# Two layers' mixer inputs, gated recurrence, pooling and difference attention put into one stage

## What is computed

```
for l in range(2):
    u = rms_norm(h, norm1_g[l])
    p_in, dq, dk, dv, gq, gk, gv, gr, gg = split(u @ w_in[l])   # 256, 512, 512, 512, 128, 128, 256, 256, 16 columns
    y_pool = (causal means of p_in over 2, 4, 8, 16 tokens - p_in) @ pool_w * pool_scale
    y_diff = rms_norm((softmax(q0 k0) - lam * softmax(q1 k1)) @ v) * gain   # 4 heads, two maps of 64, values of 128,
                                                                            # mask by blocks of 64 tokens
    y_gla  = rms_norm(chunked gated recurrence of gq, gk, gv with log decays from gg) * silu(gr)
                                                                            # 4 heads, keys 32, values 64, chunks of 64
    h = h + concat(y_pool, y_diff, y_gla) @ w_out[l]
    h = h + square(relu(rms_norm(h) @ w_mlp1[l])) @ w_mlp2[l]
```

## Time and profile before

| | |
|---|---|
| median of 3 runs | 2982.12 us (2980.08 to 2985.23) |
| the profiled execution, its own time | 2992.76 us |
| its span in the profile | 2991.0 us |
| instructions | 45324 |
| PE, DVE, ACT, POOL busy | 2706.6, 1510.7, 1001.0, 274.0 us |
| weight load part of PE (PEld) busy | 2131.9 us |
| DMA | 222.99 MB, mean 75 GB/s |

### The profile page before, as it was taken

The page is one execution under the profiler, slowest core; times in us unless marked ns, Lnnn a source line. Parts: engine busy times, 40 slices in busy tenths (PEclk is TensorE's granted clock), DMA queues, the critical chain, the costliest instruction groups (busy, mean ns, idle before and its releaser), DMA issues. The chain is left out here.

```text
span 2991.0 us, 45324 instructions
## 1 busy us (share of the span) xinstructions
PE 2706.6 (90%) x19410; PEld 2131.9 (71%) x19410; DVE 1510.7 (51%) x1980; ACT 1001.0 (33%) x1600; POOL 274.0 (9%) x217
## 2 busy tenths in 40 slices
PE   6989999799997999899999946999999966899998
PEld 4745688678886787688787834778777854687776
DVE  4654598345676233566534356552443347553443
ACT  3333575333333222333333225321222225331221
POOL 0210001312320000111111020100001020100000
PEclk8999999768999999999999978999999978999999
DMA  6224211000003233233222200223222200232322
GB/s 237 64 88 131 89 62 57 3 3 3 4 32 118 92 93 113 76 92 98 79 93 90 92 8 3 90 92 92 92 86 91 92 21 1 72 98 85 92 91 71
DMA packets 64712, 222.99 MB, mean 75 GB/s; under 512 B 7168, under 2 KB 7552, under 8 KB 64384
## 3 DMA queue, kind: packets, MB, share of 16 engines
q1 hardware_dynamic: 63360, 216.94, 22.9%
q10 hardware_dynamic: 1152, 3.15, 0.3%
HBM read 213.77 MB, written 6.29 MB: 74 GB/s over the span
## 5 line engine op out<-in xcount | busy, mean ns | idle before, releaser
L276 DVE TENSOR_TENSOR w_lo<-ring,w_hi 128x1024 fp32r<-128x1024 f32 (+1 forms) x339 | 420.9, 1242 | 984.0 <-ACT w_hi L268 983.9
L268 ACT CAST w_hi<-ring 128x1024 fp32r<-128x1024 f32 (+1 forms) x339 | 353.2, 1042 | 1115.2 <-PE ps L298 995.4
L298 PE MATMUL ps<-u_hi,w_hi 128*128 128x512 f32 x1104 | 441.0, 399 | 15.0 <-DVE u_lo L493 10.1
L298 PE MATMUL ps<-u_hi,w_lo 128*128 128x512 f32 x1104 | 437.4, 396 | 0.0
L298 PE MATMUL ps<-u_lo,w_hi 128*128 128x512 f32 x1104 | 435.7, 395 | 0.0
L298 PE MATMUL ps<-mid_hi,w_hi 128*128 128x512 f32 x688 | 275.1, 400 | 16.8 <-PEq L2609 10.6
L298 PE MATMUL ps<-mid_lo,w_hi 128*128 128x512 f32 x688 | 275.3, 400 | 0.0
L298 PE MATMUL ps<-mid_hi,w_lo 128*128 128x512 f32 x688 | 274.4, 399 | 0.0
L298 PEld LDWEIGHTS ps<-u_hi,w_hi 128*128 128x128 f32 x1104 | 208.1, 188 | 71.8 <-issue 17.7
L298 PEld LDWEIGHTS ps<-u_hi,w_lo 128*128 128x128 f32 x1104 | 208.2, 189 | 52.4
L298 PEld LDWEIGHTS ps<-u_lo,w_hi 128*128 128x128 f32 x1104 | 208.1, 189 | 49.9
(11 more groups left out here) (390 smaller groups left out, 4524.1 us busy)
## 6 DMA issues: line engine op xcount, KB each, us to landing
ring<-in_w_up SPq DMA_DIRECT2D x44, 512.0 KB, 3.5
ring<-in_w_in SPq DMA_DIRECT2D x42, 512.0 KB, 3.5
ring<-in_w_mod_rest SPq DMA_DIRECT2D x32, 512.0 KB, 3.5
ring<-in_w_merge SPq DMA_DIRECT2D x32, 512.0 KB, 3.5
ring<-in_w_mlp1a SPq DMA_DIRECT2D x32, 512.0 KB, 3.5
ring<-in_w_mlp2a SPq DMA_DIRECT2D x32, 512.0 KB, 3.5
ring<-in_w_mlp1b SPq DMA_DIRECT2D x32, 512.0 KB, 3.5
ring<-in_w_mlp2b SPq DMA_DIRECT2D x32, 512.0 KB, 3.5
```

The lines of the kernel that those rows point to most:

```text
L268: nc.scalar.copy(w_hi[:, slot, 0:width], ring[:, n % RING, 0:width]).then_inc(*hi_ok.one())
L276: nc.vector.tensor_tensor(w_lo[:, slot, 0:width], ring[:, n % RING, 0:width], as_f32(w_hi[:, slot, 0:width]), ALU.subtract).then_inc(*lo_o ...
L298: mm = nc.tensor.matmul(dst[:, a:b], w[wi][:, k * P:(k + 1) * P], src[xi][:, k0 + k, a:b], start=start and k == wi == xi == 0, stop=stop a ...
```

## The change

The three stages become one, `stage_mixer`. The units' order changes to gg, gk, gq, gv (2), dv (4), then dk and dq of each head, pool input (2), gr (2). The pieces of recurrence, attention and pooling are placed between units and between quarters of a unit on TensorE's queue: gate matmul after unit 2 (counting from 0), transposes of the decayed keys after unit 6, recurrence scores after 7, states after 8, output inside unit 10; then ten **slots**, one per unit 11 to 20, in each of which one pair of attention items starts and the pair before ends; pooling stands in the last slot.

The operations change too. Keys and queries of the recurrence are used by their 32 partitions instead of through zeroed tiles, states have 64 columns instead of 256, the score products of the attention contract over 64 partitions each and their masks cover 64 columns over 32 partitions. The attention's values come token-major, one product per item; the norms of both mixers become sums along a row (`accum_out` of a Square on ScalarE, or a reduce on VectorE) with square roots of a few columns, and the normed tiles are transposed back by TensorE through one PSUM bank (bank 2) and scaled as ScalarE takes them out. The scaling by 1/16 moves into the Exps, the probabilities take one VectorE operation instead of two, and 1/sum of map 0 is applied when the value product is taken out. Transposed probabilities, back transposes and pool mixing take turns in bank 2, value products in bank 3, scores in banks 4 to 7. On ScalarE's and VectorE's queues the steps are written out in one order with the splits: in a slot ScalarE does split, both copies of transposed probabilities, first value copy and square, Exps of the first starting item, second value copy and square, Exps of the second; VectorE scales the last product, ends the second item's probabilities, splits, takes both maxima and ends the first item's probabilities. The updates of x in layer 0 move behind the first splits. GpSimd zeroes only small tiles, and its pool means go by tile, after cumulative sums that VectorE makes in slots 7 and 8.

```diff
         for layer in range(DEPTH2):
+            part, at_unit = {}, 0
+            for kind, n in (("pin", 2), ("gq", 1), ("gk", 1), ("gr", 2), ("gg", 1), ("dq", DH2), ("dk", DH2),
+                            ("gv", 2), ("dv", 4)):
+                part[kind] = t_w[f"in2_{layer}"][at_unit:at_unit + n]
+                at_unit += n
+            by_head = [part[kind][h:h + 1] for h in range(DH2) for kind in ("dk", "dq")]
+            t_w = {**t_w, f"in2_{layer}": sum([part["gg"], part["gk"], part["gq"], part["gv"], part["dv"]] + by_head +
+                                              [part["pin"], part["gr"]], [])}
...
-        def stage_mixer_inputs(u, x, first_gain, rstd, pin, gq, gk, gr, gg, qz, dk, dv, gv):
...
-        def stage_pool_gla(layer, mats, pin, gq, gk, gr, gg, gv, mix):
...
-                        nc.gpsimd.memset(kp[:], 0.0).then_inc(*l_ok.one())
...
-                        for half in range(2):
-                            nc.vector.tensor_scalar(kt[:, half, :, :].rearrange("p t c -> p (t c)"), ps[:, 3, :],
-                                                    tab("half", half, 1), None, ALU.mult).then_inc(*d_ok.one())
...
-        def stage_diff(layer, qz, dk, dv, mix):
...
+        def stage_mixer(layer, u, x, first_gain, rstd, mats, mix):
...
+            GG, GK, GQ, HEAD = 0, 1, 2, 9
+            FIRST = HEAD + 2
+            SLOTS = n_units - FIRST
...
+                        def gla_scores():
+
+                            for t in range(TL):
+                                for h in range(4):
+                                    r = slice(32 * h, 32 * h + 32)
+                                    mm = nc.tensor.matmul(ps[:, SCORE_BANKS[h], t * P:(t + 1) * P],
+                                                          kinv[r, t * P:(t + 1) * P], gq[r, t * P:(t + 1) * P],
+                                                          start=True, stop=True)
...
+                        def gla_states():
+
+                            for c in range(NCH):
+                                t, r = c // 2, slice(64 * (c % 2), 64 * (c % 2) + 64)
+                                for h in range(4):
+                                    mm = nc.tensor.matmul(ps[32 * h:32 * h + 32, STATE_BANKS[c % 2], 64 * t:64 * t + 64],
+                                                          kt[r, t, 32 * h:32 * h + 32], gv[r, t, 64 * h:64 * h + 64],
+                                                          start=True, stop=True)
...
+                        def gla_out():
+
+                            for t in range(TL):
+                                for h in range(4):
+                                    r, dst = slice(32 * h, 32 * h + 32), ps[:, OUT_BANKS[h], 64 * t:64 * t + 64]
+                                    nc.tensor.matmul(dst, at_[:, t, h, :], gv[:, t, 64 * h:64 * h + 64],
+                                                     start=True, stop=False)
+                                    for half in range(2):
+                                        c, q = 2 * t + half, slice(64 * half, 64 * half + 64)
+                                        mm = nc.tensor.matmul(dst[q, :], gq[r, c * GLA_C:(c + 1) * GLA_C], st[r, c, :],
+                                                              start=False, stop=True)
...
+                            def product_of_map(m):
+                                r = slice(64 * m, 64 * m + 64)
+                                nc.tensor.matmul(score(i, m), dq[r, h, t * P:n], dk[r, h, 0:n], start=True, stop=False)
+
+                            def masked(m):
+                                return nc.tensor.matmul(score(i, m)[:, n - 64:n], tab("mask_q")[0:32, :],
+                                                        tab("mask_k")[0:32, 64:128], start=False, stop=True)
+
+                            product_of_map(0)
+                            product_of_map(1)
+                            masked(0)
+                            masked(1).then_inc(*s_ok.one())
...
+                        def values(i):
+
+                            h, t = divmod(i, TL)
+                            pe.wait_ge(*tev.at(i + 1))
+                            if i > 0:
+                                pe.wait_ge(*o_ok.at(i))
                             for k in range(t + 1):
+                                mm = nc.tensor.matmul(ps[:, 3, t * P:(t + 1) * P], pt[:, i % 2, k * P:(k + 1) * P],
+                                                      dv[:, k, h * P:(h + 1) * P], start=k == 0, stop=k == t)
+                            mm.then_inc(*pv_ok.one())
...
+                        for n in range(3):
+                            part(unit(pe), n, 0, KD)
...
+                        pe.wait_ge(*rs_ok.at(1))
...
+                        pe.wait_ge(*evac.at(1))
+                        nc.tensor.matmul(ps[:, 0, :], mats[0:16, layer * P:(layer + 1) * P], gg[0:16, :],
+                                         start=True, stop=True).then_inc(*p_ok.one())
...
+                            if i == 1:
+                                pe.wait_ge(*d_ok.at(9))
+                                for t in range(TL):
+                                    mm = nc.tensor.transpose(ps[:, 0, t * P:(t + 1) * P], ke[:, t * P:(t + 1) * P], ident)
+                                mm.then_inc(*p_ok.one())
+                            elif i == 2:
+                                pe.wait_ge(*evac.at(2))
+                                pe.wait_ge(*tok_evac.at(4))
+                                pe.wait_ge(*a_ok.at(6))
+                                gla_scores()
+                            elif i == 3:
+                                pe.wait_ge(*d_ok.at(11))
+                                gla_states()
+                        pe.wait_ge(*d_ok.at(13))
+                        part(unit(pe), HEAD, 0, KD)
+                        w = unit(pe)
+                        part(w, HEAD + 1, 0, 2)
+                        pe.wait_ge(*d_ok.at(20))
+                        pe.wait_ge(*tok_evac.at(8))
+                        gla_out()
+                        part(w, HEAD + 1, 2, KD)
+                        for s in range(SLOTS):
+                            n = FIRST + s
+                            ending, starting = items_ending(s), items_starting(s)
+                            w = unit(pe)
+                            pe.wait_ge(*evac.at(feature(n) - 1))
+                            part(w, n, 0, 2)
+                            if ending:
+                                turn(ending[0])
+                            part(w, n, 2, 4)
+                            if starting:
+                                scores(starting[0])
+                            if ending:
+                                turn(ending[1])
+                                values(ending[0])
+                            elif s == SLOTS - 1:
+                                pool_mix(0)
+                            part(w, n, 4, 6)
+                            if starting:
+                                scores(starting[1])
+                            if ending:
+                                values(ending[1])
+                            elif s == SLOTS - 1:
+                                pool_mix(1)
+                            part(w, n, 6, KD)
+                            if s in (2, 4):
+                                gla_back((s - 2) // 2)
+                            elif s % 2 == 1 and s > 1:
+                                head_back((s - 3) // 2)
...
-                    with ExitStack() as s3:
...
-                        stage_mixer_inputs(u, x, (lambda n: vec("final", n)) if layer == 0 else None, rstd,
-                                           pin, gq, gk, gr, gg, qz, dk, dv, gv)
-                        normed.close()
-                        stage_pool_gla(layer, mats, pin, gq, gk, gr, gg, gv, mix)
-                        stage_diff(layer, qz, dk, dv, mix)
+                    stage_mixer(layer, u, x, (lambda n: vec("final", n)) if layer == 0 else None, rstd, mats, mix)
+                    normed.close()
```

More of the change, by code:

```diff
@@ L2455, in _, with part @@
                     @block.tensor
                     def _(pe):
-                        pe.wait_ge(*lam_ok.at(1))
-                        nc.tensor.matmul(ps[:, 7, 0:2], ones, lam[:, 0:2], start=True,
-                                         stop=True).then_inc(*lams_ok.one())
+                        def part(w, n, k0, k1):
+                            for k in range(k0, k1):
+                                for wi, xi in ((0, 0), (0, 1), (1, 0)):
+                                    mm = nc.tensor.matmul(ps[:, bank(n), :], w[wi][:, k * P:(k + 1) * P], u[xi][:, k, :],
+                                                          start=k == wi == xi == 0, stop=k == KD - 1 and wi == 1)
+                            if k1 == KD:
+                                mm.then_inc(*unit_used.one())
@@ new lines, in head_back, with pool_mix @@
+                        def head_back(h):
```

(31 more changed lines are left out.)

783 lines of the change are left out of this document (371 added, 412 removed).

## The result

| | before | after |
|---|---|---|
| median, runs taken side by side | 2982.25 us (2980.08 to 2985.23, 4 runs) | 2842.34 us (2837.21 to 2846.40, 4 runs) |
| the profiled execution, its own time | 2992.76 us | 2841.74 us |
| its span | 2991.0 us | 2840.0 us |

The ratio of after to before is 0.9529, 95% interval 0.9512 to 0.9547: faster, as predicted, 139.9 us by the medians against the 151.6 forecast. The two profiled executions differ by 151.0 us.

A forecast was written before the change was run, and what follows sets the result against it. Bound: latency of VectorE and ScalarE chains leaving TensorE idle and half-clocked. Per layer 123.0 + 36.7 + 16.1 + 7 + 1.6 = 184.4 us against 260.2; two layers save 151.6, giving 2830.5 us, own range 2800 to 2860.

The forecast's parts named there:

- The quarter units: In the ten slots, each dependent piece stands a quarter unit or more behind its source, so the chain fits, narrowly.
- to take the whole difference from one median: Whole kernel: the 151.6 us saved in two layers is subtracted from the median before, 2982.1, giving 2830.5 us.
- the output: Recurrence output per layer: 16 matmuls over 128 rows and 32 small ones, taken as 6.5 us, between 4.1 and 9.4.
- Attention, 36.7 forecast: TensorE time of all attention pieces per layer: 36.7 us, between 26.0 and 41.9.
- I take 3/4: 13.0: Attention score products per layer: 17.4 us without overlap, 8.7 with the two maps side by side; 13.0 taken for partial pairing.
- Recurrence, 16.1 forecast: TensorE time of the recurrence pieces, with gate and pool mixing, per layer: 16.1 us, between 9.7 and 23.7.
- I put at 6 us: Joined stage, per layer: about 90 added TensorE waits and the tile changes cost 6 us, 7 with the pool's exposed time.
- drains: Rival, chance 0.12: about 84 tile changes a layer cost 0.16 us each, 13.4 us instead of 6; 2845 us in all.
- Full overlap: Rival, chance 0.08: tiles run side by side everywhere, pieces 35.7 us and waits 2, 22.1 us less a layer; 2786 us.
- The rows show low clocks only with idle PE: Ground against a halved clock in the joined stage: the profile before showed low clocks only where TensorE was idle.
- half clock: Rival, chance 0.03: clock stays at 1.2 GHz over twelve units from the first head on; stage 290.4 us, 3043 in all.
- About 1 us exposed: Slots 7 and 8: the pool's cumulative sums on VectorE ahead of probabilities leave about 1 us of wait per layer.

The follow-up runs named there:

- after_again: The changed kernel run once more without any edit, as reference for the other runs: 2836.95 us, ratio 0.9503 against the kernel before.

## Why the prediction was right, and where it was not

- **The mechanism held.** Chain latencies vanished behind units: the earlier trace rows are gone, PE is idle for 5.4 of 185.8 us (2.3 of them the tail), and the run with the attention's units first gives back 46 to 50 us per layer through waits and the clock. The quarter units, which the forecast leaned on for the waits, turned out not to be needed.
- **Why the medians give 140 and the stages 149.** The stages lose 148.8 us, the forecast said 151.6, and the two profiled executions differ by 151.0. The medians differ by less, 139.9, since the profiled execution of the kernel before lies 10.6 us above its median and that of the kernel after 0.6 below. Where unprofiled executions differ no trace shows; in the profiled ones the first stage starts anywhere from 1595.4 to 1607.9 us with the same code in front. Beside after_again the medians differ by 150.8. The step that failed there was to take the whole difference from one median; what the stages gain is known far better than the total.
- **The sum is better than its terms.** It is off by 1.4 us per stage, 185.8 against 184.4, but the output by +7.2, weight matmuls with start and tail by +4.1, masks by +3.2, waits by -3.9, recurrence scores and states by -3.6, transposes and values by -3.4. That these cancel so well is luck.
- **Attention, 36.7 forecast, 35.4 measured**, by two errors that cancel. "I take 3/4: 13.0" was wrong as a reading of the overlap: the maps overlap fully. Rows 5 give 8.7 us for them so; the other 3.2 are 16 x 0.20 us for the changes of tile size around them. The masks, 6.2 at 0.195 each, measured 9.4: besides the change of size, the second mask waits for the first on the same 32 rows (the run with masks on 64 rows). Transposes (4.2) and values (8.3) came a little cheaper than 5.2 and 10.0.
- **Recurrence, 16.1 forecast, 18.6 measured.** Scores and states were near the lower bound (1.9 against 5.5). The output was the mis-sized term: 13.7 instead of 6.5, above its upper bound of 9.4. 16 x 0.62 = 9.9 us of it are there at full clock, 4.7 of them owed to the order of its products, and 3.8 are the halved clock.
- **"I put at 6 us" the waits and tile changes, 7 with the pool's.** Waits were 3.1. The changes cost more than the rest of it: 3.2 us stand in the score products, up to 4.7 in the output, and the first weight matmul after a piece takes a step of 0.33 us (1660.76 to 1661.09) where most take 0.23. That last cost had no term at all, and it is not only a matter of tile size, since the transposed keys, over 128 rows, leave it too (0.32 us from 1647.26 on). With the 1.9 us of the low clock taken off, the 504 weight matmuls took 5.9 us more than 504 steps of 0.234 (5.62 us for 24).
- **The rival "drains"** was right in its mechanism. The earlier trace rows had been read as showing no drain, from starts that overlap modelled ends; what counts is the step, and that grows by 0.10 us per change around the score products and by 0.15 into the 128-row matmuls of the output. The Trainium skill, TensorEngine Tiling (Array Packing), section Tiling Modes, says that a change of mode drains the engine; the runs agree in that each change costs time, and give it that price; they show the step, not a drain itself. Its 2845 came out nearest to 2842, but through the scatter above: by stages it asked for 7.4 us a layer more than the forecast, 191.8, and 185.8 were measured, nearer to 184.4. Full overlap, the rival on the other side, held at the same time for the score products and for the recurrence's scores and states.
- **"The rows show low clocks only with idle PE"** was wrong as a ground against the rival "half clock". Here the clock fell with PE busy without a pause, in a run of small products only. The place was one run of pieces, not twelve units, so it cost 5.7 us a layer (3.8 + 1.9).
- **"About 1 us exposed" in slots 7 and 8**: 2.9 us. The cause was not the scans ahead of the probabilities, which leave no wait once the means are short, but GpSimd's means, which were called on no path that sets the end. They are on none, but they slow VectorE's, which is.
- VectorE (95.7 us in layer 1) and ScalarE (89.7) came out near the 100 and 95 forecast, the tail (2.9 us from the end of the last weight matmul on) near 3.0.

## What to carry to other kernels

A latency-bound stage is worth folding into one that streams weights: it costs the pieces' own TensorE time and hardly more, and a whole unit between them is fine enough. Then order the pieces by tile size, put independent products on different row halves next to each other, and look at the granted clock wherever only small products follow one another, however busy TensorE looks. A stage's price is best read from stage to stage in the profile, not from one total.

## What was not expected of the hardware

- The clock went to 1.2 GHz while PE was busy 13.60 of 13.60 us, 3.9 us into a run of small fp32 products (3.3 in layer 1), and stayed low for 4.0 us of weight matmuls behind them. In the eight profiles that have the output so, it falls in both stages, 2.8 to 6.0 us into it and for 10.2 to 17.1 us. With the same work grouped, in 5.24 us, it fell in none of six stages (three profiles), and in four parts between weight matmuls not within the output. Which property of these products does it was not tried further.
- Two fp32 products on different halves of the rows take as long as one (0.64 and 0.63 us at 256 columns); products on 32 rows and 64 columns go at 0.019 us per instruction when they stand together.
- GpSimd beside VectorE stretches those VectorE operations that read two tensors from SBUF: 0.22 to 1.29 us for one column, 0.75 to 1.83 for 512, 1.22 to 2.29 for 1024. A reciprocal beside it, with one input, took 0.16 (1765.98), as it does alone (0.17). The stretching is not certain for each operation: with the late scans one of the 1024-column ones beside GpSimd kept its 1.23 us. The Trainium skill, GPSIMD Engine Reference, section Specifications, names this contention for two SBUF inputs; the rows agree.
